# Expert results added to tokens by one-hot products on TensorE instead of accumulating scatters

## What is computed

```python
def moe_swiglu(h, router_w, w_gu, w_down):
    logits = jnp.einsum('bsd,de->bse', h, router_w, preferred_element_type=jnp.float32)
    top_v, top_i = lax.top_k(logits, EXPERT_TOPK)
    probs = jax.nn.softmax(top_v, axis=-1)
    gate = jnp.einsum('bsk,bske->bse', probs,
                      jax.nn.one_hot(top_i, N_EXPERTS, dtype=jnp.float32))
    y = jnp.zeros_like(h)
    for e in range(N_EXPERTS):
        y = y + gate[..., e:e + 1].astype(h.dtype) * swiglu(h, w_gu[e], w_down[e])
    return y
# x = x + moe_swiglu(rms_norm(x, ffn_norm), ...);  each expert: 1024 -> 2 x 2816 -> 1024
```

## Time and profile before

| | |
|---|---|
| median of 3 runs | 1243.8 us (1243.68 to 1244.6) |
| the profiled execution | 1245.33 us, its span 1243.5 us |
| TensorE busy | 1181.4 us (95%) |
| VectorE, ScalarE, GpSimd busy | 420.8, 381.7, 105.8 us |
| DMA | 379.02 MB, mean 305 GB/s |
| TensorE's granted clock, mean over the span | 0.995 |

### The profile page before, as it was taken

How to read it: one execution, slowest core, us unless ns; L and a number is a source line. 1 busy time by engine, 2 the same in 40 slices (tenths; PEclk the granted TensorE clock), 3 DMA queues, 4 the chain that set the end, 5 groups by cost and what they waited for, 6 DMA issues and landing times.

```text
span 1243.5 us, 27148 instructions
## 1 busy us (share of the span) xinstructions
PE 1181.4 (95%) x12184; PEld 744.6 (60%) x12184; DVE 420.8 (34%) x700; ACT 381.7 (31%) x641; POOL 105.8 (9%) x106
## 2 busy tenths in 40 slices
PE   9999999999999999999999999999999999777775
PEld 7877788888889877786444444444444444333322
DVE  4786666645446776564111011101100101000000
ACT  6698836434337697831000000000000000000000
POOL 0520000000002220000100200201002001010000
PEclk9999999999999999999999999999999999999999
DMA  8743545755536533579999999999999999999994
GB/s 277 219 133 103 179 160 168 238 174 198 168 120 225 191 102 113 193 301 425 421 424 422 403 422 415 405 423 406 412 422 400 423 424 406 425 411 424 424 415 178
DMA packets 76525, 379.02 MB, mean 305 GB/s; under 512 B 7690, under 2 KB 14132, under 8 KB 51828
## 3 DMA queue, kind: packets, MB, share of 16 engines
q1 hardware_dynamic: 71872, 369.99, 76.2%
q0 software_dynamic: 3888, 5.11, 1.9%
q10 hardware_dynamic: 644, 2.12, 0.4%
HBM read 372.35 MB, written 4.85 MB: 303 GB/s over the span
## 4 chain that ended last, share of the span: by engine, by line
PE 81%; DMA 12%; SPq 4%; ACT 2%; issue 1%; DVE 0%; POOL 0%; POOLq 0%; ACTq 0%; DVEq 0%
PE ps L1263 26%; PE ps L772 12%; PE ps L774 12%; PE ps L773 12%; PE ps L1280 12%; DMA s_unit<-in_experts_dram 9%; SPq L713 4%; DMA m_unit<-in_experts_dram 3%; PE ps L904 1%; PE ps L957 1%; PE ps L897 1%; PE ps L893 1%; PE ps L930 1%; ACT w_hi L1387 1%; ACT mix L1377 1%
## 5 line engine op out<-in xcount | busy, mean ns | idle before, releaser
L1263 PE MATMUL ps<-s_unit,eT 128*32 128x352 f32 x3936 | 301.4, 460 | 19.7 <-DMA s_unit<-in_experts_dram 19.7
L1733 DVE TENSOR_TENSOR w_lo<-raw,w_hi 128x2048 fp32r<-128x2048 f32 (+3 forms) x93 | 197.2, 2126 | 111.2 <-ACT w_hi L1387 110.5
L1263 PEld LDWEIGHTS ps<-s_unit,eT 128*32 128x32 f32 x3936 | 117.8, 110 | 192.3 <-issue 156.2
L1387 ACT CAST w_hi<-raw 128x2048 fp32r<-128x2048 f32 (+3 forms) x93 | 165.6, 1784 | 119.6 <-PE ps L774 107.6
L772 PE MATMUL ps<-w_hi,hT_hi 128*128 128x512 f32 (+1 forms) x464 | 179.7, 387 | 1.6 <-DVE w_lo L2009 0.9
L774 PE MATMUL ps<-w_hi,hT_lo 128*128 128x512 f32 (+1 forms) x464 | 176.4, 380 | 0.0
L773 PE MATMUL ps<-w_lo,hT_hi 128*128 128x512 f32 (+1 forms) x464 | 175.9, 379 | 0.0
L1675 ACT ACTIVATE e_act<-ps 128x352 f32<-128x352 f32 x42 | 19.5, 463 | 508.7 <-PE ps L1263 508.7
L1280 PE MATMUL ps<-s_unit,hidT 128*32 128x256 f32 x1936 | 119.5, 384 | 10.5 <-DMA s_unit<-in_experts_dram 10.5
L2145 DVE TENSOR_TENSOR e_act<-e_act,ps 128x352 f32<-128x352 f32 x42 | 21.2, 504 | 299.4 <-ACT e_act L1675 298.3
L1263 PE MATMUL ps<-m_unit,eT 128*32 128x352 f32 x1440 | 110.4, 460 | 7.9 <-DMA m_unit<-in_experts_dram 7.9
(11 more groups left out here) (219 smaller groups left out, 1150.8 us busy)
## 6 DMA issues: line engine op xcount, KB each, us to landing
s_unit<-in_experts_dram SPq DMA_DIRECT2D x128, 1408.0 KB, 15.4
m_unit<-in_experts_dram SPq DMA_DIRECT2D x64, 1408.0 KB, 14.9
raw<-in_w_in_dram SPq DMA_DIRECT2D x28, 1024.0 KB, 5.3
raw<-in_dense_w_gate_up_dram SPq DMA_DIRECT2D x20, 1024.0 KB, 5.2
raw<-in_dense_w_down_dram SPq DMA_DIRECT2D x9, 1024.0 KB, 4.8
raw<-in_w_out_dram SPq DMA_DIRECT2D x8, 1024.0 KB, 4.8
raw<-in_w_in_dram SPq DMA_DIRECT2D x8, 672.0 KB, 4.7
raw<-in_w_branch_a_dram SPq DMA_DIRECT2D x4, 1024.0 KB, 5.1
```

What stands on the lines that cost most here:

```text
L1263: last = pe.matmul(ps[2 * g + gu][strip(q), 0:PIECE], eT[:, g, STRIP * b:STRIP * (b + 1)], unit[:, at:at + PIECE], start=b == 0, stop=b == ...
L1387: act.copy(w_hi[u % SPLIT][:, 0:SIZE[u]], raw[u % RAW][:, 0:SIZE[u]]).then_inc(hi_ready, 1)
L1733: dve.tensor_tensor(w_lo[q][:, 0:m], raw[u % RAW][:, 0:m], w_hi[q][:, 0:m].bitcast(F32), ALU.subtract).then_inc(split, 1)
```

## The change

x is no longer stored before item 0. It stays in SBUF, and the results are added to it there. For each item, VectorE builds a one-hot matrix for each group (`spread`: slot by token, 128 partitions x 256 tokens, from the slots' token numbers and the constant row `token_no`). TensorE multiplies: stationary `spread` of a strip (32 slots x 128 tokens), moving `y_rows` of that strip (32 slots x 256 columns), summed over the groups, into PSUM bank s for strip s; two halves of tokens share a bank. That is 8 products a group, four at a time on the four row strips of the array (`spread_group`). For item i - 1 this is done in `down_e(i, 0)`, ahead of its fifth of 11 steps (`SPREAD_AT = 4`), after a wait for `hidden_e(i, 1)` to have read the banks. VectorE then adds the four banks to x (`add_rows`, four operations of 128 x 2 x 256), and the next `gate_up_e` waits for that. GpSimd's scatters go, with `rows_kept`, `rows_now` and `rows_landed`. At the end SyncE stores x to `out` in two DMAs of 512 KB, each after its half of the additions.

```diff
+SPREAD_AT = 4
...
-        o = part(3 * GROUPS)
-        gate_next, gate_kept, gate_now = (mix[:, o + GROUPS * j:o + GROUPS * (j + 1)] for j in range(3))
+        o = part(5 * GROUPS)
+        gate_next, gate_kept, gate_now, token_next, token_kept = (mix[:, o + GROUPS * j:o + GROUPS * (j + 1)] for j in range(5))
+        o = part(T)
+        token_no = mix[:, o:o + T]
...
+        spread = over("spread", [P, GROUPS, T], hT_at + 4 * GROUPS * PIECE, F32)
...
                     load_late(k * NEXP, 0)
                     with sp.Fori(1, NEXP) as e:
                         load_late(e + k * NEXP, e)
+            for half in range(2):
+                cols = slice(half * 512, (half + 1) * 512)
+                sp.wait_ge(rows_added, last * 2 + (half + 1))
+                sp.dma_start(out[0, :, cols].rearrange("(t p) c -> p t c", p=P), x[:, :, cols]).then_inc(x_out, 16)
+            sp.wait_ge(x_out, 16 * 2)
...
                                 pe.wait_ge(first_dve, 1)
                         elif b == 0:
                             pe.wait_ge(hid_done, stage_ahead(i, c, g))
+                            if c == 0 and g == 0 and ordinary(i):
+                                if i > 1:
+                                    pe.wait_ge(rows_added, 2 * (i - 1))
                             if c == 0:
                                 pe.wait_ge(eT_set, groups_before(i) + (g + 1 - GROUPS))
                         for gu in range(2):
...
                             pe.wait_ge(y_out, groups_before(i))
                         places(i + 2)
+            def spread_group(i, g):
+                for t in range(NT):
+                    for s in range(STRIPS):
+                        last = pe.matmul(ps[s][:, t * QUARTER:(t + 1) * QUARTER], spread[strip(s), g, t * P:(t + 1) * P],
+                                         y_rows[strip(s), g, :], start=g + t == 0, stop=g == groups_of(i) - 1, skip_group_check=True)
+                return last
+            def spread_rows(i):
+                pe.wait_ge(spread_set, i + 1)
+                for g in range(groups_of(i)):
+                    pe.wait_ge(y_out, groups_before(i) + (g + 1))
+                    last = spread_group(i, g)
+                last.then_inc(spread_done, 1)
             def down_block(i, c, k, g, s, arriving):
                 u, blk = divmod(STRIPS * k + s, E_BLOCKS)
...
                 n = groups_of(i)
                 for k in range(KT_D):
+                    if k == SPREAD_AT and c == 0 and ordinary(i) and i:
+                        pe.wait_ge(hid_done, stage_no(i, 1, n - 1))
+                        spread_rows(i - 1)
                     for g in range(n):
                         if k == 0:
                             pe.wait_ge(hidT_set, stage_no(i, c, g))
...
                 gate_up_e(i, 1)
                 down_e(i, 0)
             down_last(NEXP - 1, 1)
+            spread_rows(NEXP - 1)
...
             act.activation(r16[4], r16[0], ACT.Exp).then_inc(route_exp, 1)
             act.activation(ss_h[:, 0, :], r16[0].rearrange("p t e -> p (t e)"), ACT.Silu)
             keep_rows(1)
-            act.dma_start(out[0].rearrange("(t p) c -> p t c", p=P), x[:, :, :]).then_inc(x_out, 16)
             for i in range(NEXP):
                 silu_e(i, 0)
                 if i:
...
                     for c in range(PIECES):
                         silu_e(i, c)
                     results(i)
-            act.wait_ge(rows_added, last * (16 * GROUPS) + 16 * (GROUPS + LATE_LESS))
-            act.copy(r2[0], r2[1])
         @block.vector
...
                 dve.tensor_copy(staged_, route[:, :, bass.ds(column, 1)].rearrange("p q i -> p (q i)")).then_inc(staged, 1)
                 dve.wait_ge(staged, n_staged)
-            def places_now(i, rows, gate):
-                dve.wait_ge(rows_landed, i + 1)
+            def places_now(i, token, gate):
                 dve.wait_ge(meta_next, i + 1)
-                dve.tensor_copy(rows_now[:, :], rows[:, :])
                 dve.tensor_copy(gate_now, gate).then_inc(meta_now, 1)
+                for g in range(groups_of(i)):
+                    last = dve.tensor_scalar(spread[:, g, :], token_no, token[:, g:g + 1], None, ALU.is_equal)
+                last.then_inc(spread_set, 1)
             def keep_places(i):
                 dve.wait_ge(meta_next, i + 1)
                 if i:
                     dve.wait_ge(meta_now, i)
-                dve.tensor_copy(rows_kept[:, :], rows_next[:, :])
+                    dve.wait_ge(spread_set, i)
+                dve.tensor_copy(token_kept, token_next)
                 dve.tensor_copy(gate_kept, gate_next)
+            def add_rows(i):
+                dve.wait_ge(spread_done, i + 1)
+                for half in range(2):
+                    for q in (2 * half, 2 * half + 1):
+                        xs = x[:, :, q * QUARTER:(q + 1) * QUARTER]
+                        last = dve.tensor_tensor(xs, xs, view(q, NT, QUARTER), ALU.add)
+                    last.then_inc(rows_added, 1)
             def places_next(i):
...
                 dve.wait_ge(meta_turned, i + 1)
                 by_group = meta_T.rearrange("p (g i) -> p g i", g=GROUPS)
                 dve.tensor_scalar(rows_next[:, :], by_group[:, :, 0], float(STRIPS), con("strip_no"), ALU.mult, ALU.add)
+                dve.tensor_copy(token_next, by_group[:, :, 0])
                 dve.tensor_copy(gate_next, by_group[:, :, 1]).then_inc(meta_next, 1)
             def one_hot(column, n_staged):
...
                     one_hot_next(i + 1)
                 hidden_e(i, 0)
                 if i:
-                    places_now(i - 1, rows_kept, gate_kept)
+                    places_now(i - 1, token_kept, gate_kept)
                 else:
                     places_next(0)
                     dve.wait_ge(order_known, 1)
...
                     places_next(i + 1)
                     gathered(i + 1)
                 hidden_e(i, 1)
+                if i:
+                    add_rows(i - 1)
             gathered_first()
...
             for t in range(NT):
                 last = dve.tensor_tensor(route[:, 3 + 2 * t, at:at + NEXP], chosen[:, t, :], ex[:, t, :], ALU.mult)
             step(last)
+            for n, w in ((0, CAP), (CAP, CAP), (2 * CAP, T - 2 * CAP)):
+                last = dve.tensor_scalar(token_no[:, n:n + w], slot_no[:, 0:w], float(n), None, ALU.add)
+            step(last)
             for i in range(NEXP):
                 item(i)
-            places_now(NEXP - 1, rows_next, gate_next)
+            places_now(NEXP - 1, token_next, gate_next)
+            add_rows(NEXP - 1)
             last = dve.value_load(last_item[0:1, 0:1], min_val=NEXP - 1, max_val=ITEMS - 1)
             with dve.If(last > NEXP - 1):
                 with dve.Fori(NEXP, ITEMS) as i:
                     one_hot(i + 1, i + 1)
                     dve.wait_ge(meta_now, i)
+                    dve.wait_ge(spread_set, i)
                     places_next(i)
                     gathered(i)
-                    places_now(i, rows_next, gate_next)
+                    places_now(i, token_next, gate_next)
                     for c in range(PIECES):
                         hidden_e(i, c)
+                    add_rows(i)
         @block.gpsimd
...
                     pool.indirect_dma_start(x_rows[:, g, :], None, h_quarters,
                                             bass.IndirectOffsetOnAxis(rows_next[:, g:g + 1], 0)).then_inc(rows_in, 16)
-            def add_rows(i):
-                if i:
-                    pool.wait_ge(rows_added, 16 * groups_before(i))
-                pool.sem_inc(rows_landed, 1)
-                for g in range(groups_of(i)):
-                    pool.wait_ge(y_out, groups_before(i) + g + 1)
-                    pool.indirect_dma_start(out_quarters, bass.IndirectOffsetOnAxis(rows_now[:, g:g + 1], 0), y_rows[:, g, :], None,
-                                            compute_op=ALU.add).then_inc(rows_added, 16)
             pool.wait_ge(h_out, 16 * NT)
-            pool.wait_ge(x_out, 16)
             for i in range(1, NEXP):
                 fetch(i)
-                add_rows(i - 1)
-            add_rows(NEXP - 1)
             pool.wait_ge(items_known, 1)
             last = pool.value_load(last_item[0:1, 0:1], min_val=NEXP - 1, max_val=ITEMS - 1)
             with pool.If(last > NEXP - 1):
                 for i in range(NEXP, ITEMS):
                     fetch(i)
-                    add_rows(i)
 _INS = ["x", "attn_norm", "w_in", "moba_q_norm", "moba_k_norm", "mla_cq_norm", "w_uq", "mla_ckv_norm", "w_ukv",
```

More of the change, by code:

```diff
@@ L477, in trunk @@
         last_item = over("last_item", [1, 1], ints, I32)
-        rows_next, rows_kept, rows_now = (over(n, [P, GROUPS], ints + 32 * (j + 1), I32)
-                                          for j, n in enumerate(("rows_next", "rows_kept", "rows_now")))
-        order = over("order", [1, NEXP - 1], ints + 128, I32)
+        rows_next = over("rows_next", [P, GROUPS], ints + 32, I32)
```

(9 more changed lines are left out.)

## The result

| | before | after |
|---|---|---|
| median of 20 executions each, us | 1243.64 (1242.3 to 1245.28) | 1245.96 (1244.41 to 1247.53) |
| ratio, 95% interval | | 1.0019 (1.0012 to 1.0026) |
| profiled execution, us | 1245.33 | 1245.9 |
| its span, us | 1243.5 | 1244.0 |

The change makes the kernel 2.3 us slower. That is 0.19%, within what I had set as no change, and inside the range (1238 to 1250), but the sum said 1.7 us faster. The sign is wrong by 4 us, and the two profiled executions differ by only 0.5 us. So two questions are open: where the sum failed, and why the pair of profiles shows less than the medians do.

A forecast was written before the change was run, and what follows sets the result against it. TensorE sets the pace in items 0 to 4, the DMA from item 5. Loads ending 3.7 us earlier and an end 2.0 us longer give -1.7 us: median 1242.1 us, range 1238 to 1250.

The forecast's parts named there:

- unit 127 lands 6.1 us and not 15.3 us after its issue: Weight load at the start of item 5: with scatters and early store gone, the queue shortens, 9.2 us gained.
- Rival C: Mechanism holds, ends dearer: a starved load lands after 8 us, the last store takes 5.7 us; 1246 us, chance 0.20.
- the late base: The profiled execution of before that the sum started from: 1245.33 us, 1.5 us above the median of 1243.8.
- A second term: From unit 127's landing to the last landing: 219.4 us for 64 units, plus 2.0 us of fetches and small traffic.
- Rival D: Scatters displaced less than their share, 0.62 us each; moves the sum by 1.4 us, counted within the forecast's 0.55.
- the four spreads: One-hot products on TensorE in items 1 to 4, not hidden: 2.8 us each, 11.2 us together.
- The tail: After the last down products: products, additions and second store in series, landing at 1243.7, end at 1245.5, 2.0 us longer.
- P: The forecast's theory: TensorE sets the pace up to item 5, where added work counts in full; afterwards the DMA does.
- Q: Rival B as a theory in the experiments: the DMA is the bound all along and TensorE's work is covered.
- Rival B: The DMA is the bound all along, so all traffic removed counts: 1227.7 us, chance 0.07.
- Rival A: Row strips do not overlap four ways: 6.6 us a spread, 26.4 for four, about 1260 us, chance 0.18.
- near 7 us in items 3 and 4: Sign that would show the forecast: units' time from issue to landing in these items, against 14 us before.

The follow-up runs named there:

- e0: The kernel before, with nothing edited, run again: 1244.15 us, ratio 1.0000, span of its profiled execution 1242.7 us.
- e1: The kernel before without its accumulating scatters, so expert results never reach the output: 1229.14 us, ratio 0.9882 to the kernel before.
- e5: The changed kernel with item 3's spread and additions moved from the first to the second down piece of item 4: 1243.99 us, ratio 0.9996 to before.
- e6: The changed kernel with spreads of items 0 to 3 kept in SBUF and made in batches in items 5 and 6: 1234.37 us, ratio 0.9924 to before.
- e9: The changed kernel with each one-hot product made five times: 1297.93 us, ratio 1.0435 to the kernel before.
- e3: The changed kernel with each one-hot product made twice: 1258.34 us, ratio 1.0117 to the kernel before.
- e4: The changed kernel with the early 1 MB store of x put back: 1246.2 us, ratio 1.0017 to the kernel before.
- e2: The changed kernel with only the last group's one-hot products of each item, waits and additions kept: 1239.63 us, ratio 0.9966 to the kernel before.
- e7: The changed kernel with the one-hot products in float32r, one record a product instead of two: 1236.82 us, ratio 0.9940 to the kernel before.
- e8: The changed kernel with both late spreads (e6) and float32r products (e7): 1233.07 us, ratio 0.9914 to the kernel before.

## Why the prediction was wrong, and where it was right

**The step that failed** is "unit 127 lands 6.1 us and not 15.3 us after its issue": 9.2 us gained. I had taken the least of 192 landing times as that of a starved queue. It is that of a load alone. At TensorE's pace two or three loads are under way, and unit 127 took about 8.4 us in the changed kernel, 2.3 us more than I had put in. Other kernels agree. All landings of unit 127 below are read from the traces, except that of the changed kernel:

| | unit 127 issued, us | landed after, us | from there to the last landing, us |
|---|---|---|---|
| before, first profile | 990.4 | 15.3 | 227.1 |
| before again (e0) | 990.0 | 14.3 | 227.3 |
| without scatters (e1) | 989.7 | 8.8 | 222.7 |
| changed | 1002.0 | 8.4 (estimate) | 222.4 |
| one spread moved (e5) | 998.5 | 8.8 | 222.1 |
| spreads late (e6) | 990.1 | 9.5 | 221.9 |

The floor of 8 to 9 us is there with no products, with late ones and, in e9, with five times as many. The step was also too large at its other end: 15.3 us belongs to a late execution, and e0 has 14.3. From e0 to the changed kernel this gain is 5.9 us, not 9.2. Rival C had the floor, and its 1246 is the measured time, but partly by luck: its other half, 2.2 us for a dear store, did not come in the changed kernel (3.5 us, as I had put it), and the late base made up for it. In e3, e4, e5 and e9 the same last store took 4.7 to 5.0 us; no run says why.

**A second term**: from the landing of unit 127 to the last I had 219.4 + 2.0 us, and it took 222.4, 1.0 us more. By the last column the seven scatters were worth 5.0 us and not 5.7 (4.4 to 5.4 over these kernels), 0.7 us each. Rival D of the forecast, that a scatter displaces less than its share, had the direction right, with 0.62.

**A smaller miss**: the four spreads cost 12.3 us, not 11.2. The products themselves are exact, 2.80 us against 2.8. The rest is the 0.14 us in the down piece around each spread and the 0.17 us in three gate-up pieces, for which no row names a cause. As the expert stage began 0.7 us earlier, unit 127 was issued 0.4 us later than forecast.

**The tail was over-priced**: +0.5 us, not +2.0. I had carried 1.8 us from the last landing to the end over from the old program, where ScalarE's copy follows the scatter. After the last store only 0.4 us follow. The additions took 2.48 us, not 2.75. This error hid part of the others.

**The base was late.** Against the first profiled execution the terms close: -1.7 + 2.3 + 1.0 + 0.4 - 1.5 = +0.5, the difference of the spans. So these terms explain 2.2 of the 4.0 us by which the forecast of the median was off. The other 1.8 us are the base: I took the changed kernel's profiled execution to be 1.5 us above its median, as that of before was, and it was not. Against e0 the last unit reads: unit 127 is issued 12.0 us later, lands 5.9 us faster, and 5.0 us of scatters are gone, together the 1.1 us by which the last unit lands later.

**Where the gain went.** It was there: e1 took 14.8 us off the kernel by removing the scatters alone. The change takes 12.3 of it back on TensorE in the four items where TensorE is the pace. At the end nothing is left of the 4.5 us that e1 gains there, as products, additions and stores take the scatters' place. An edit to a kernel with two bounds, one after the other, was good for the second and bad for the first; e6 keeps the good half.

**What held.** P, against Q: more or fewer products moved the time nearly one for one (e3 by 12.4 us for 12.1, e2 by 6.3 for 6.9, e9 by 52.0 for 48.3), and traffic before item 5 moved nothing (e4). Rival B, 0.07, is dead. Rival A, 0.18, is dead as well: four row strips overlap. 48 records one after another at 0.215 us, an estimate from the earlier trace rows, would be 10.3 us, so the overlap is 3.7 times. The Trainium skill (TensorE: Matmul & The Clock Gate, Part 3, Measured speedup vs the span model) has 3.07 times, for products with 512 moving columns; an estimate by it would be 3.4 us for a spread. The measured 2.80 us decides against it for this stream, with 256 columns. The Trainium skill (TensorEngine Tiling (Array Packing), Key Properties) says that a change of mode drains the array; the 0.2 us that e3 shows to be paid once for a spread would fit, but no run here isolates it. Also as forecast: no wait of TensorE up to 1040 us, additions hidden in items 1 to 6, and the full queue again after item 6 (37.0 us to land).

Not as forecast: the landing time did not come near 7 us in items 3 and 4 (8.1 and 8.8).

**Left open**: whether the floor of 8 to 9 us is a queue that forms anew in each item or the price of loads under way together, the 0.3 us an item around the spread, and why the last store takes 3.1 to 3.7 us in some profiled executions and 4.7 to 5.0 in others. Executions of one kernel differ by 3 us over 20.

## What to carry to other kernels

Where one engine sets the pace in the first part of a program and a transfer in the second, work moved onto that engine costs its full length in the first part and next to nothing in the second: put it there (9.9 us faster than before, against 2.3 slower), even if results must be kept for a while. Bandwidth freed ahead of the point where the pace changes is worth only the queue that it shortens, and the floor of that queue is to be read from loads with as many others under way, not from the shortest of all. Where an effect of 2 us is worked out against one profiled execution, look at a second one first.

## What the runs showed of the hardware that I had not expected

- A load of 1408 KB that is alone lands in 5.7 to 6.3 us (e9, after each of four pauses from 740 to 1037 us). After the last two of these pauses the next loads took 7.1 to 7.2 and then 8.0 us; after that it stays at 7.7 and more, while the DMA's share is near 1.0.
- A pause of 2.8 us on TensorE, at some 9 us of landing time, left 11 us at 313 GB/s, 2.8 us of transfer missing; a pause of 8 us at a longer queue left nothing missing.
- Float32r products of 32 rows by 256 columns took 0.92 us for 24 records, float32 ones 2.80 us for 48: three times for twice the records.
- In the changed kernel the two stores of 512 KB landed in 2.9 and 3.5 us. The second, with the first still under way, took 3.1 to 3.7 us in four more kernels (e2, e6, e7, e8) and 4.7 to 5.0 us in e3, e4, e5 and e9.
